# Two stacked blocks on one core: the second block's input projections as three products of rounded parts

## The reference, cut to what matters

```python
def second_block(x, meta_tokens, w_in, ...):
    h = jnp.concatenate([meta, x], axis=1)                 # 16 + 256 = 272 tokens
    for l in range(DEPTH):                                 # DEPTH = 2
        proj = h @ w_in[l]                                 # 1024 x 4176
        dq, dk, dv, dz, db, da, sq, sk, sv, iq, ik, iw = jnp.split(proj, SPLIT_POINTS, axis=-1)
        o_dn = deltanet_group(dq, dk, dv, dz, db, da, conv_w[l], a_log[l], dt_bias[l], dn_norm_g[l])
        o_sa = dsa_group(sq, sk, sv, iq, ik, iw, cos, sin, cos_i, sin_i, k_top)
        mix = jnp.concatenate([o_dn, o_sa.astype(o_dn.dtype)], axis=-1) @ w_out[l]
        h = layer_norm(DEEPNORM_ALPHA * h + mix, ln1_g[l], ln1_b[l])
        ffn = hier_moe(h, w_grp[l], b_grp[l], w_rtr[l], b_rtr[l], w1[l], w3[l], w2[l])
        h = layer_norm(DEEPNORM_ALPHA * h + ffn, ln2_g[l], ln2_b[l])
    return h[:, N_META:]

def deltanet_group(q, k, v, z, ...):
    qkv = jax.nn.silu(causal_dwconv(jnp.concatenate([q, k, v], -1), conv_w))   # width 4, per feature
    q, k = l2norm(q), l2norm(k)                            # per head of 128
    ...                                                    # chunked delta rule, norm, * silu(z)

def dsa_group(q, k, v, qi, ki, wi, ...):
    ...                                                    # rotary embedding of q, k, qi, ki
    rel = jax.nn.relu(jnp.einsum('bqhd,bsd->bqhs', qib, ki) * IDX_DH ** -0.5)
    score = jnp.einsum('bqhs,bqh->bqs', rel, wib)
    _, sel = lax.top_k(score, k_top)                       # 64 keys per query
    ...                                                    # softmax attention over them
```

## Time and profile before

| | us |
|---|---|
| median of 3 runs | 2222.85 |
| their lowest and highest | 2222.04, 2228.54 |
| the profiled execution | 2216.83 |
| its span, first to last instruction | 2215.0 |

### The profile page before, as it was taken

The page is one execution under the profiler, slowest core; times in us unless marked ns, Lnnn a source line. Parts: engine busy times, 40 slices in busy tenths (PEclk is TensorE's granted clock), DMA queues, the critical chain, the costliest instruction groups (busy, mean ns, idle before and its releaser), DMA issues.

```text
span 2215.0 us, 36775 instructions
## 1 busy us (share of the span) xinstructions
PE 2023.3 (91%) x14355; PEld 1623.4 (73%) x14359; DVE 941.3 (42%) x1872; ACT 743.5 (34%) x1186; POOL 698.0 (32%) x558
## 2 busy tenths in 40 slices
PE   7989999999999999999999986859999999879866
PEld 6779899998889999987768763424678587734423
DVE  5562436606633456327744341112277443512212
ACT  5554443345645443422322121212223122222212
POOL 6557648885666568810011000000000020000000
PEclk9999999999999999999999998979999899899978
DMA  7335335563444355453300369997433102697794
GB/s 226 99 112 171 115 127 183 177 190 106 133 134 154 113 171 186 157 173 116 114 39 1 152 280 418 421 421 275 152 115 115 39 1 115 254 386 311 296 420 166
DMA packets 196268, 405.94 MB, mean 183 GB/s; under 512 B 18515, under 2 KB 143846, under 8 KB 171286
## 3 DMA queue, kind: packets, MB, share of 16 engines
q1 hardware_dynamic: 192374, 390.20, 48.2%
q0 software_dynamic: 3744, 13.63, 1.6%
HBM read 400.53 MB, written 3.28 MB: 182 GB/s over the span
## 4 chain that ended last, share of the span: by engine, by line
PE 73%; DMA 7%; DVE 7%; ACT 4%; SPq 3%; issue 2%; DVEq 2%; ACTq 1%; POOL 1%; POOLq 0%
PE ps L1000 10%; PE ps L1001 9%; PE ps L1002 9%; PE ps L1331 9%; PE ps L1671 6%; DMA weight_ring<-in_w 5%; SPq L910 3%; PE ps L1693 3%; PE ps L1582 3%; PE ps L1074 2%; DMA last_pair<-in_w 1%; DVEq L2205 1%; PE ps L1529 1%; PE ps L1428 1%; PE ps L1701 1%
## 5 line engine op out<-in xcount | busy, mean ns | idle before, releaser
L2162 POOL TENSOR_TENSOR weight_ring<-weight_ring 128x512 fp32r<-128x512 f32 (+1 forms) x466 | 629.6, 1386 | 318.1 <-ACT weight_ring L1767 298.9
L1000 PE MATMUL ps<-weight_ring 128*128 128x256 f32 x1824 | 531.9, 292 | 20.4 <-DVE acts L2279 8.4
L1002 PE MATMUL ps<-weight_ring 128*128 128x256 f32 x1568 | 442.4, 282 | 0.0
L1001 PE MATMUL ps<-acts,weight_ring 128*128 128x256 f32 x1472 | 418.2, 284 | 0.0
L1000 PEld LDWEIGHTS ps<-weight_ring 128*128 128x128 f32 x1824 | 347.9, 191 | 34.4 <-issue 27.8
L1002 PEld LDWEIGHTS ps<-weight_ring 128*128 128x128 f32 x1568 | 301.3, 192 | 0.0
L1001 PEld LDWEIGHTS ps<-acts,weight_ring 128*128 128x128 f32 x1472 | 281.8, 191 | 1.9 <-issue 1.4
L1767 ACT ACTIVATE weight_ring<-weight_ring 128x2048 fp32r<-128x2048 f32 x128 | 238.7, 1883 | 84.9 <-PE ps L1002 75.6
L1331 PE MATMUL ps<-acts,weight_ring 128*128 128x272 f32 x896 | 211.1, 394 | 2.8 <-ACTq L2112 1.4
L2184 POOL CAST row_of<-slot_token 128x1 uint32 (+1 forms) x26 | 4.8, 185 | 639.9 <-PE ps L1649 427.4
L1331 PEld LDWEIGHTS ps<-acts,weight_ring 128*128 128x128 f32 x896 | 169.3, 190 | 40.3 <-issue 2.4
(11 more groups left out here) (459 smaller groups left out, 3746.5 us busy)
## 6 DMA issues: line engine op xcount, KB each, us to landing
weight_ring<-in_w SPq DMA_DIRECT2D x120, 1024.0 KB, 23.0
weight_ring<-in_w_gate_up SPq DMA_DIRECT2D x44, 1024.0 KB, 5.1
acts<-in_w SPq DMA_DIRECT2D x40, 1024.0 KB, 25.4
weight_ring<-in_w_in SPq DMA_DIRECT2D x16, 2048.0 KB, 9.2
weight_ring<-in_x_wkv SPq DMA_DIRECT2D x16, 1024.0 KB, 5.3
weight_ring<-in_w_down SPq DMA_DIRECT2D x16, 1024.0 KB, 5.0
h_area<-in_w SPq DMA_DIRECT2D x16, 1024.0 KB, 21.5
last_pair<-in_w SPq DMA_DIRECT2D x16, 1024.0 KB, 24.5
```

What stands on the lines that cost most here:

```text
L1000: nc.tensor.matmul(o, wh, xh, start=start, stop=False)
L1001: nc.tensor.matmul(o, wh, xr, start=False, stop=False)
L1002: return nc.tensor.matmul(o, wr, xh, start=False, stop=stop)
L2162: nc.gpsimd.tensor_tensor(r12(w), w, r12(high[:, n % HIGH, part]).bitcast(F32), ALU.subtract).then_inc(rest_ready, 1)
```

## The change

For each layer, `hT` is split too: ScalarE casts it in two halves to the rounded `hH` (in `oT`), VectorE makes `hL = hT - hH` (in `work`). The seven chunks other than `iq` are cut into fourteen halves of 256 columns, `HALVES`, each loaded into one of five bays (`half_raw`: bays 2, 3, 4, 5, 1). `half_highs(q)` on ScalarE writes its high part to one of three (`half_high`: bays 6, 7, 0), GpSimd makes the rest in place, in four instructions of 512 columns, and TensorE waits for the quarter that it needs (`half_rest`). High part q waits for the last tile that reads half q - 3, load q for that of half q - 5. `iq`, `ik` and the narrow columns stay as they are.

```diff
+        hH = oT
+        hL = work[:, 2 * S2:2 * S2 + KT * S2].rearrange("p (k t) -> p k t", k=KT)
+        half_raw, half_high = [bays[:, b] for b in (2, 3, 4, 5, 1)], [bays[:, b] for b in (6, 7, 0)]
+        HALVES = [(nm, h) for nm in ("dq", "dk", "dv", "dz", "sq", "sk", "sv") for h in range(2)]
...
-            for turn_, nm in enumerate(("iq", "dq", "dk", "dv", "dz", "sq", "sk", "sv")):
-                if l == 0 and turn_ == 2:
+            chunk(("iq", l), [(0, 8, 512, cols(w2in, SPLIT["iq"], SPLIT["iq"] + 512))], lasts["iq"], slot=0)
+            for q, (nm, h) in enumerate(HALVES):
+                if l == 0 and q == 2:
                     chunk_order.append(("second", None, None))
-                chunk((nm, l), [(0, 8, 512, cols(w2in, SPLIT[nm], SPLIT[nm] + 512))], lasts[nm], slot=turn_ % 4)
+                if q < 4:
+                    release = entry[(1, 1, 2, 2)[q]]
+                else:
+                    release = lasts["iq"] if q == 4 else half_last[14 * l + q - 5]
...
+            def project_split(key, l, q, i):
+
+                b = begin(*key)
+                if q == 0 and i == 0:
+                    pe.wait_ge(u_ready, 24 + 2 * (l + 1))
+                w, wh = half_raw[q % 5], half_high[q % 3]
+                for k in range(KT):
+                    if i == 0:
+                        half_rest(l, q, k)
+                    at = slice(k * 256 + i * P, k * 256 + i * P + P)
+                    last = split_products(ps[:, b, 0:S2], (r12(wh[:, at]), r12(w[:, at])), (r12(hH[:, k, :]), r12(hL[:, k, :])),
+                                          start=(k == 0), stop=(k == KT - 1))
+                last.then_inc(full[b], 1)
+
+            def values_split(key, l, t0, tn):
+
+                b = begin(*key)
+                for q in (12, 13):
...
+                        last = split_products(ps[0:tn, b, 256 * (q - 12):256 * (q - 11)], (r12(hH[:, k, t0:t0 + tn]), r12(hL[:, k, t0:t0 + tn])),
+                                              (r12(wh[:, at]), r12(w[:, at])), start=(k == 0 and q == 12), stop=(k == KT - 1 and q == 13))
...
                     if m % 6 == 5:
-                        project2(("c", l, m // 6), weights("dq", l), m // 6 * P, 512)
-                for nm, at in PROJ[1:]:
-                    s = weights(nm, l)
-                    for i in range(4):
-                        project2(("c", l, at + i), s, i * P, 512)
+                        project_split(("c", l, m // 6), l, m // 12, m // 6 % 2)
+                for i in range(4, 16):
+                    project_split(("c", l, i), l, i // 2, i % 2)
...
+                def half_highs(q):
+
+                    key = ("d", 1, 3) if l == 0 else ("mu", 0, 1)
+                    b, u = tiles[key if q < 2 else ("proj", l, "iq", 3) if q == 2 else half_last[14 * l + q - 3]]
+                    act.wait_ge(full[b], u)
+                    act.wait_ge(loaded[1 + q % 5], half_loads[14 * l + q])
+                    nc.scalar.activation(r12(half_high[q % 3]), half_raw[q % 5], ACT.Copy).then_inc(high_ready, 1)
...
             for l in range(DEPTH):
+                for q in range(14):
+                    pool.wait_ge(high_ready, len(bay_order) + 14 * l + q + 1)
+                    for a in range(4):
+                        w = half_raw[q % 5][:, 512 * a:512 * a + 512]
+                        nc.gpsimd.tensor_tensor(r12(w), w, r12(half_high[q % 3][:, 512 * a:512 * a + 512]).bitcast(F32),
+                                                ALU.subtract).then_inc(rest_ready, 1)
...
+                for a in range(2):
+                    half = slice(4 * a, 4 * a + 4)
+                    dve.wait_ge(uh_ready, 24 + 2 * l + a + 1)
+                    nc.vector.tensor_tensor(r12(hL[:, half, :]), hT[:, half, :], r12(hH[:, half, :]).bitcast(F32), ALU.subtract).then_inc(u_ready, 1)
```

More of the change, by code:

```diff
@@ L261, in build @@
         row_sum = rot2_tmp[:, :]
-        work = sb("work", [P, 3072], stack=middle)
+        work = two_views("work", [P, 3072], stack=middle)
         middle.close()
@@ L784, in build @@
                 lasts[nm] = ("c", l, at + 3)
[L785 to L788 removed]
+            for nm, at in PROJ:
+                half_last.extend(("c", l, at + 2 * h + 1) for h in range(2))
+            half_last.extend(("proj", l, nm, 2 * h + 1) for nm in ("sq", "sk") for h in range(2))
+            half_last.extend([("sv", l, 2)] * 2)
+            entry = list(last_tile)
+            chunk(("iq", l), [(0, 8, 512, cols(w2in, SPLIT["iq"], SPLIT["iq"] + 512))], lasts["iq"], slot=0)
+            for q, (nm, h) in enumerate(HALVES):
+                if l == 0 and q == 2:
+                    chunk_order.append(("second", None, None))
+                if q < 4:
+                    release = entry[(1, 1, 2, 2)[q]]
+                else:
+                    release = lasts["iq"] if q == 4 else half_last[14 * l + q - 5]
+                slot_loads[1 + q % 5] += 16
+                half_loads.append(slot_loads[1 + q % 5])
+                chunk_order.append(("half", cols(w2in, SPLIT[nm] + 256 * h, SPLIT[nm] + 256 * h + 256), release, q))
+            for s_ in range(SLOTS):
+                last_tile[s_] = half_last[14 * l + 11]
             take("gcc", l)
@@ L890, in _ @@
             for slot, parts, last, *more in chunk_order:
+                if slot == "half":
+                    q, = more
+                    b, u = tiles[last]
+                    sp.wait_ge(full[b], u)
+                    sp.dma_start(half_raw[q % 5].rearrange("p (k n) -> p k n", k=KT), parts).then_inc(loaded[1 + q % 5], 16)
+                    continue
                 if slot == "second":
@@ L1333, in project2, with half_rest @@
                 last.then_inc(full[b], 1)
+            def half_rest(l, q, k):
+                pe.wait_ge(rest_ready, 4 * len(bay_order) - len(by_vector) + 4 * (14 * l + q) + k // 2 + 1)
+            def project_split(key, l, q, i):
[13 more added lines that the diff above has]
+                for q in (12, 13):
+                    w, wh = half_raw[q % 5], half_high[q % 3]
+                    for k in range(KT):
+                        if t0 == 0:
+                            half_rest(l, q, k)
+                        at = slice(k * 256, k * 256 + 256)
+                        last = split_products(ps[0:tn, b, 256 * (q - 12):256 * (q - 11)], (r12(hH[:, k, t0:t0 + tn]), r12(hL[:, k, t0:t0 + tn])),
+                                              (r12(wh[:, at]), r12(w[:, at])), start=(k == 0 and q == 12), stop=(k == KT - 1 and q == 13))
+                last.then_inc(full[b], 1)
             def each_head(key, fn):
@@ L1975, in _ @@
             for l in range(DEPTH):
+                def half_highs(q):
[5 more added lines that the diff above has]
+                for a in range(2):
+                    if l == 1:
+                        act.wait_ge((ln_low, ln_done)[a], 2)
+                    half = slice(4 * a, 4 * a + 4)
+                    nc.scalar.activation(r12(hH[:, half, :]), hT[:, half, :], ACT.Copy).then_inc(uh_ready, 1)
+                half_highs(0)
                 projected = [t for t in rot_tiles(INDEX) if t[0] == "proj"]
@@ L2023, in _ @@
                                  scale=0.125 if nm == "sq" else 1.0)
+                        if i % 2 and (nm, i) != ("sk", 3):
+                            half_highs((11 if nm == "sq" else 13) + i // 2)
                 for n, (t0, L) in enumerate(TOK):
```

16 lines of the change are left out of this document (13 added, 3 removed).

## The result

The changed kernel takes 2268.6 us (median of four runs, 2267.58 to 2270.0); the kernel before, in four runs, 2225.69 (2222.04 to 2231.85). The ratio is 1.0198, with a 95% interval of 1.0182 to 1.0214: 43 us slower. The profiled execution took 2269.05 us, with a span of 2267.2. The direction was forecast, the size was not: 2250 was the forecast, and 2268.6 lies 2.6 us beyond the upper end of its range.

A forecast was written before the change was run, and what follows sets the result against it. Up to `qs` TensorE and VectorE both bound the kernel, and GpSimd's rests delay VectorE. Per layer 16.3 - 3.9 + 1.9 = 14.3 us, twice 28.6, on 2216.83 gives 2245.4; with the median 6.0 higher, 2250 us, range 2220 to 2266.

The forecast's parts named there:

- What bounds the kernel: Up to the copy of `qs`, TensorE and VectorE finish within 3 us; delaying VectorE by over about 2 us moves the end.
- A product's price: TensorE's split tiles: a product of 272 columns takes 0.124 us, so a tile takes 2.98 us and saves 0.70.
- Rival C: TensorE's products of 272 columns take 0.23 us, not 0.124, so TensorE alone bounds the stretch: 2303 us; chance 4%.
- A: GpSimd hardly holds up VectorE's convolutions, so the change makes the kernel faster: 2209 us; chance 11%.
- B: GpSimd's rests hold up VectorE's top-k too, up to 16 us more a layer: 2282 us; chance 6%.
- D: Rests fall mostly in the top-k or in waits, so collisions and gains cancel: 2218 to 2230 us; chance 8%.
- The collisions in the convolutions: Rests of halves 8 to 10 meet VectorE's convolution work: 12 rests at 1.0 us each, +12 us a layer.
- The resume: TensorE resumes at `qs` 1.3 us after the convolutions' end rather than 3.0, taking 1.7 us off a layer.
- The scores: Rests of halves 2 and 3 meet score products: 8 us, of which about 2 are hidden, so +6 a layer.
- Behind `qs`: Six tiles save 4.2 us, set against 12 rests of halves 11 to 13 that meet VectorE's rotations and scalings: 0.
- The values: TensorE's value tiles: 144 products of 256 columns take 17.0 us for 20.9, -3.9 us a layer.
- The sum: Per layer 16.3 - 3.9 + 1.9 for lost clock = 14.3 us, twice 28.6 us, all passed on to the total.

## Why the prediction was wrong in its size

**What bounds the kernel: right.** "what TensorE gives back before that point is worth nothing unless VectorE gets there earlier too, and whatever delays VectorE by more than about 2 us moves the end." The run with four products per step shows the first half, the runs without rests the second. (The run of 15 tiles from 1017.35, which I called feature tiles, is 13 of these and two of `sq`; the sum had them right.)

**A product's price: right.** Twenty-four products take 3.03 us from start to start (1060.97 to 1064.00), 0.126 each for a forecast of 0.124. Rival C is out, and so are A (collisions happen) and B (the top-k takes 23.7 us as before). D didn't happen.

**The collisions in the convolutions: right in size, by one half off in place.** Forecast +12, measured 12.3 from the top-k's start to the convolutions' end. The 12 rests of halves 8 to 10 are 11.0 of it (the convolutions end at 90.2 without them, at 101.2 with them), 0.92 each; 1.3 are the last rests of half 7, which reached beyond the top-k. That the two errors nearly cancel is luck. The rests of half 10 were over with the third of the twelve tiles. The price per rest, 1.0 us forecast, was 0.8 to 1.1 in the rows.

**The resume: right.** Forecast 1.3 us behind the convolutions' end, measured 0.8.

**The scores: mis-sized, 8.6 for +6.** The step that failed is "of which the waits of 1.83 and 1.72 us there and the tiles' 2 us hide about 2". Four of the eight rests did not fall into the scores at all but on the last index rotation and on gate operations of 12 columns, where nothing hides them: (1.37 - 0.44) + (1.25 - 0.17) + (1.24 - 0.17) + (1.14 - 0.17) = 4.05 us, the 4.1 by which the scores begin late. The trace of before shows these operations at 0.17 us, and I took them as too small to count; beside a rest of 512 columns an operation of 12 columns loses as much as one of 272. The other four rests cost 5.50 - 2.22 = 3.3 us. And the wait of 1.83 did not shrink but grew to 4.67, most of it through TensorE's half clock, told above (without these rests it is 2.29). Only the wait of 1.72 was used up: 4.05 + 3.3 + 2.84 - 1.72 = 8.5. The run without these rests gives 10.1 us a layer back.

**Behind `qs`: the mechanism right, the price left out.** "VectorE frees the rotations' banks before the values can start, so I set these against each other: 0." Bounded by VectorE it was. But VectorE's way from the first rotation to the one that frees the values' bank took 30.3 us (1094.10 to 1124.36), 27.1 before (1074.81 to 1101.91), because of the rests, while TensorE, faster by its six tiles, arrived early and stood for 3.98 us. From `qs` to the values' start are 32.1 us, 29.7 before: +2.4, for a forecast of 0 + 1.9 (clock).

**The values: mis-sized, -1.0 for -3.9.** Their products are as short as forecast at full clock: from 1131 on a group of 24 takes 2.85 us. But the first 6 us ran at the half clock that TensorE's wait brought (columns of the earlier trace rows; after):

```profile
1124.90:1131.00 6.10, 6.10 (x29) 6.10 (x30) 5.35 (x14) 0.00 (x0) 0.00 (x0) 0.50 1.05 388
1131.00:1144.60 13.60, 13.60 (x117) 12.52 (x117) 0.27 (x1) 1.20 (x2) 0.00 (x0) 1.00 0.10 37
```

Values of 19.8 us instead of 17.0 are about half of those 6, and the run without the rests of halves 11 to 13, whose wait there is 1.68 us, has them at 17.1 with the clock at 1.00. This is the second step that failed: the -3.9 was entered without a clock cost. I had counted the clock for the wait for `qs` and for no other: the wait ahead of the values was in my own sum, as the saving that VectorE would not let through, and I did not ask what a wait does to the clock of the work behind it.

**The sum.** Forecast per layer 16.3 + 1.9 - 3.9 = 14.3; found 19.1 + 2.4 - 1.0 = 20.5 (the table's 20.3). The miss of 6 is 2.6 in the scores and 2.9 in the values, and the small ones. From 2250 to 2268.6 are 18.6 us: twice 6 is 12; the median of before is 2.8 higher over four runs than over the three that I had; 1.4 I had rounded off; the last 2.4 lie outside the table's stretch, where two executions differ by more than that, and no run says what they are. The upper bound of the range took neither term in: it stretched the price per rest, not the number of places where a rest hurts.

## What to carry to other kernels

A lockout by a GpSimd instruction of 512 columns cost about the same whether it caught a long operation of VectorE or one of 12 columns, so work handed to GpSimd is costed by how many of its instructions meet such work, and is laid beside sorting, reciprocals or waits, or cut into shorter instructions. Time given back to an engine that then waits is not neutral, since its next work can run at the half clock: fill the wait with real work (here the value tiles) before making the product faster. The split that lost 43 us over all weights gained 21 to 24 over the halves whose rests had a free place.

## What the runs showed of the hardware

- GpSimd and VectorE took turns on two-input work in SBUF, one instruction each. VectorE's loss per full turn was 0.8 to 1.1 us beside 512 columns (GpSimd 1.29), and less where its operation came late in a rest. Beside 256 columns (0.74) it was 0.32 for the convolutions' operations and 0.30 to 0.54 for four of 12 columns.
- TENSOR_SCALAR with both ends in SBUF was locked out as well, down to 12 columns (0.17 to 1.25 us); MAX8 and MATCH_REPLACE8 were not (23.7 us of top-k beside 14 rests, 23.8 without), nor was RECIPROCAL (1.85 us each, six of sixteen beside rests).
- A wait of TensorE of 2.56 us was followed by 7 us near the half clock, one of 3.98 us by 6 us of it; one of 1.68 us at the same place by none (1.00). Idle products through a wait of 21 us kept the clock at 1.00 through the wait and behind it.
- Two profiles of the unchanged kernel differ by 11 us of span, 10 of it between the delta rule's start and the experts; stages are compared by their own rows, not by the span.
